# State-space phase: order and buffering of the gate units' store, powers of the scan in PSUM, large levels in two pieces

## The chip, the cores and the metric

One Trainium2 chip; the kernel runs on one core of it. The metric is the device time of one execution in microseconds (us). Five engines take part: PE (TensorE: matmuls, with its weight loads shown as PEld), DVE (VectorE), ACT (ScalarE), POOL (GpSimd) and SP (SyncE), which here does nothing but wait on semaphores and issue DMA transfers in a fixed order.

## What is computed

The reference is a model of two blocks on 256 tokens of width 1024. The change lies in one part of the first block, its second layer, an S5 state-space mixer over 256 context tokens and then 256 tokens, in both directions:

```python
def s5_scan(u, abar, bbar, cmat, h0):            # per chunk of the sequence
    def step(h, u_blk):
        bu = jnp.einsum('btgn,gpn->btgp', u_blk.astype(jnp.complex64), bbar)
        bu = bu.at[:, 0].add(abar[None] * h)
        a = jnp.broadcast_to(abar, bu.shape)
        _, hs = lax.associative_scan(_linrec_combine, (a, bu), axis=1)   # h[t] = abar * h[t-1] + bu[t]
        y = jnp.einsum('btgp,gnp->btgn', hs, cmat).real
        return hs[:, -1], y
```

`u` is one half of a projection of the modulated, normalised input (`s5_w_in`, 1024 x 4096); the other half, z, goes through SiLU and later multiplies the mixer's output (after GELU and a gated linear unit). There are 128 groups of 16 channels with 64 complex states each. All is fp32: a product is made from three matmuls, lead x lead, lead x rest and rest x lead, where `lead` is the operand rounded to the matmul's format (an ACT copy) and `rest` what remains (a DVE or POOL subtraction).

## The kernel before, in words

`s5_mixer` (from line 1538) runs the phase as five programs, one for each engine, tied together by semaphores. All five count the same steps n = 0 to 26 (`STEPS` = 27), and the order of work inside a step is written out by hand. The 16 channel tiles (k = 0 to 15, 128 channels each) run through a pipeline of stages that lie some steps apart:

- Step n below 16: TensorE projects unit n of u (`project`, L1767: 8 x 3 matmuls of 128x512) into `ps_u`; ACT copies it to `us`; SP stores it and loads it back turned as `ub`. Steps 16 to 23: the units are the gate's z, two units of 256 columns in a step (`gate_half`, 24 matmuls each), both into `ps_u`; ACT puts them through SiLU into `zb` (L1962), and SP stores `zb` (L1687). The unit's weights come from the ring: ACT makes `w_lead` (`lead`, L1885), DVE `w_rest` (`rest`, L1990), two buffers of each.
- Step n, tile n - 2 (`BACK`): TensorE makes the states' inputs (L1868) into `ps_s`, ACT spreads them into `S` (L1955 to L1957).
- Tile n - 9 (`LAG`): TensorE makes the lag kernels (L1790 to L1803) from V, which POOL builds (L1751 to L1753, twelve instructions for a tile) or, for five tiles, SP loads; ACT evicts them (L1921), SP turns them by four loads into T (L1668).
- Tile n - 10 (`OUT`): ACT copies the scanned states to `hs` (`states`, L1900, L1901), TensorE makes the outputs (L1819) from hs, V, T and `ul`; every second tile ACT applies GELU, every fourth step TensorE turns four tiles (`turn_outputs`) and ACT copies them on (`gate_inputs`).

The scan itself is DVE's. The tiles go in four quarters q = 0 to 3 of four tiles; `scan(q, part)` runs parts 0 to 3 in steps 6 + 4q to 9 + 4q. A scan goes up and down a tree of 5 levels over 64 chunk states; each move is one `advance` with four instructions: L2001 and L2002 multiply states by powers of abar (real part; imaginary part with crossed components), L2003 adds the two into `t1`, L2004 adds the sum to the states.

`apow` (powers), `S` (states) and `t2` lie in SBUF, `t1` in PSUM (two banks). A scan's advances have, in order, 1024, 960, 960, 448, 192, 64, 64, 128, 256, 512 and 1024 elements per partition, 5632 together. Between the two halves of parts 0 to 2, and behind both halves of part 3, stand the `w_rest` of the next step's units. `scanned` is raised at a scan's end, and ACT's `states` of the quarter wait for it.

SP's order in a step before: store of u, T loads (behind the lag eviction of this step), loads of W and ub, the units' weights, and only then the store of z of the step before; ACT's SiLU waits for that store, as `zb` is one buffer.

The phase begins with `ModulatedParts`: eight tiles of the input are turned by TensorE into a ring of PSUM banks (L628), ACT makes `h_lead` (L635), DVE the value (L645), POOL `h_rest` (L652). The ring has six banks, four borrowed from `ps_s` and `ps_y` and two from `t1`; the tiles that don't fit are turned between the matmuls of unit 0.

## Time and profile before

| | |
|---|---|
| time, median of 3 runs | 1713.45 us (1709.28, 1713.45, 1713.57) |
| the profiled execution | 1709.84 us, span 1707.8 us |
| busy: PE, PEld, DVE, ACT, POOL | 91%, 78%, 58%, 46%, 39% |
| granted TensorE clock, mean | 0.952 of full speed |
| the state-space phase | about 553 to 899 us of the span |
| moved by DMA | 328.8 MB, mean 193 GB/s |

The durations used below come from the profiled execution, whose times count from the start of its span. "Granted clock" is the share of full speed that TensorE was given in a stretch. "Idle before" is the time in which an engine did nothing before an instruction, with the instruction that ended the wait.

### The profile page before, as it was taken

The numbers are of one execution on the slowest core, as the hardware profiler recorded it, in microseconds if no ns is written. First come the engines' busy times: TensorE is split into PE (matmuls) and PEld (weight loads), VectorE is DVE, ScalarE is ACT, GpSimd is POOL, SyncE is SP. The second block draws the span as 40 slices with busy tenths as digits, with TensorE's granted clock in tenths as the row PEclk, the third lists the DMA queues.
The fourth block names the chain that finished last, engine by engine and source line by source line (L and its number), as shares of the span: only waits on it lengthen the run. The fifth ranks groups of instructions, "written<-read, shape, count | busy, mean of one in ns | idle before, by whom it ended". The sixth has DMA issues, their size and how long they took to land. (4 is left out here: it accounts for less than half of the span.)

```text
span 1707.8 us, 28308 instructions
## 1 busy us (share of the span) xinstructions
PE 1552.7 (91%) x11434; PEld 1327.3 (78%) x11434; DVE 995.4 (58%) x1271; ACT 791.2 (46%) x1064; POOL 664.3 (39%) x505
## 2 busy tenths in 40 slices
PE   4799999799699899998579998989999999899998
PEld 0478888588688788787569987778999967689997
DVE  6444532388735358669826645564766655557665
ACT  2422222365412577675354434554545464455452
POOL 0089994599698943478902015111000000110000
PEclk9889999999899999989779999889999999899999
DMA  9976775466534677877657455315535333245531
GB/s 386 427 273 230 247 251 192 143 194 194 202 125 169 179 251 195 226 209 224 154 152 273 173 187 185 148 50 198 222 149 220 123 114 148 99 162 209 220 149 50
DMA packets 119289, 328.80 MB, mean 193 GB/s; under 512 B 33396, under 2 KB 72692, under 8 KB 102920
## 3 DMA queue, kind: packets, MB, share of 16 engines
q1 hardware_dynamic: 116310, 301.71, 51.7%
q10 hardware_dynamic: 2868, 25.54, 4.2%
q8 instruction: 79, 1.29, 0.3%
q14 instruction: 32, 0.26, 0.1%
HBM read 282.17 MB, written 36.65 MB: 187 GB/s over the span
## 5 line engine op out<-in xcount | busy, mean ns | idle before, releaser
L3033 PE MATMUL ffn_ps<-ffn_x_lead,w_lead 128*128 128x256 f32 x672 | 188.4, 280 | 1.1 <-DVE w_rest L3112 1.1
L3033 PE MATMUL ffn_ps<-ffn_x_lead,w_rest 128*128 128x256 f32 x672 | 188.6, 281 | 0.0
L3033 PE MATMUL ffn_ps<-ffn_x_rest,w_lead 128*128 128x256 f32 x672 | 188.3, 280 | 0.0
L401 POOL TENSOR_TENSOR w_rest<-resident_ring,w_lead 128x2048 fp32r<-128x2048 f32 x7 | 32.1, 4590 | 394.9 <-ACT w_lead L397 206.3
L3112 DVE TENSOR_TENSOR w_rest<-resident_ring,w_lead 128x2048 fp32r<-128x2048 f32 x42 | 96.1, 2292 | 83.7 <-ACT w_lead L3077 83.7
L365 PE MATMUL qkvz_ps<-qkvz_w_lead,h_lead 128*128 128x512 f32 x320 | 125.8, 393 | 5.8 <-POOL h_rest L652 5.8
L3033 PEld LDWEIGHTS ffn_ps<-ffn_x_lead,w_lead 128*128 128x128 f32 x672 | 126.1, 188 | 2.2 <-issue 1.4
L3033 PEld LDWEIGHTS ffn_ps<-ffn_x_rest,w_lead 128*128 128x128 f32 x672 | 126.4, 188 | 0.7
L3033 PEld LDWEIGHTS ffn_ps<-ffn_x_lead,w_rest 128*128 128x128 f32 x672 | 126.3, 188 | 0.0
L365 PE MATMUL qkvz_ps<-qkvz_w_lead,h_rest 128*128 128x512 f32 x320 | 125.4, 392 | 0.0
L365 PE MATMUL qkvz_ps<-qkvz_w_rest,h_lead 128*128 128x512 f32 x320 | 125.4, 392 | 0.0
L1767 PE MATMUL ssm_ps_u<-h_lead,w_lead 128*128 128x512 f32 (+1 forms) x256 | 94.1, 368 | 33.8 <-DVE w_rest L1990 22.8
L282 DVE TENSOR_TENSOR qkvz_w_rest<-resident_ring,qkvz_w_lead 128x2048 fp32r<-128x2048 f32 x20 | 55.4, 2771 | 118.6 <-ACT qkvz_w_lead L276 118.6
L282 DVE TENSOR_TENSOR w_rest<-resident_ring,w_lead 128x2048 fp32r<-128x2048 f32 x33 | 77.3, 2344 | 71.0 <-ACT w_lead L276 70.6
L276 ACT ACTIVATE qkvz_w_lead<-resident_ring 128x2048 fp32r<-128x2048 f32 x20 | 38.5, 1923 | 149.1 <-PE qkvz_ps L365 146.9
L1428 POOL TENSOR_TENSOR resident_x<-xc,resident_x 128x512 f32<-128x512 f32 x64 | 104.9, 1640 | 5.0
L3077 ACT ACTIVATE w_lead<-resident_ring 128x2048 fp32r<-128x2048 f32 x42 | 80.1, 1912 | 50.6 <-PE ffn_ps L3033 50.5
L276 ACT ACTIVATE w_lead<-resident_ring 128x2048 fp32r<-128x2048 f32 x33 | 63.2, 1914 | 85.5 <-PE odd_ps L365 28.5
L1990 DVE TENSOR_TENSOR w_rest<-resident_ring,w_lead 128x1024 fp32r<-128x1024 f32 x32 | 48.3, 1515 | 82.7 <-ACT w_lead L1885 81.8
L1767 PE MATMUL ssm_ps_u<-h_rest,w_lead 128*128 128x512 f32 (+1 forms) x256 | 89.9, 351 | 0.0
L1767 PE MATMUL ssm_ps_u<-h_lead,w_rest 128*128 128x512 f32 (+1 forms) x256 | 89.8, 351 | 0.0
L1767 PEld LDWEIGHTS ssm_ps_u<-h_lead,w_lead 128*128 128x128 f32 x256 | 52.7, 206 | 45.8 <-issue 30.2
(534 smaller groups left out, 4506.7 us busy)
## 6 DMA issues: line engine op xcount, KB each, us to landing
resident_ring<-in_ffn_gu SPq DMA_DIRECT2D x22, 2048.0 KB, 9.0
ffn_wd<-in_ffn_down SPq DMA_DIRECT2D x22, 1024.0 KB, 4.9
resident_ring<-in_ada_w SPq DMA_DIRECT2D x8, 2048.0 KB, 13.3
xc<-s_q_scratch SPq DMA_DIRECT2D x128, 128.0 KB, 3.4
resident_x<-in_s_bT SPq DMA_DIRECT2D x64, 256.0 KB, 3.9
resident_ring<-in_attn_w_in ACTq DMA_DIRECT2D x8, 2048.0 KB, 10.4
s_W_scratch<-resident_x SPq DMA_DIRECT2D x64, 256.0 KB, 2.9
resident_ring<-in_s_w SPq DMA_DIRECT2D x32, 512.0 KB, 6.4
```

Of the source, the lines that this page charges most:

```text
L276: self.core.nc.scalar.activation(self.w[0][j], self.core.tile(r)[:, j * HK:(j + 1) * HK, :], ACT.Copy).then_inc(self.lead_made, 1)
L282: self.core.nc.vector.tensor_tensor(self.w[1][j], self.core.tile(r)[:, j * HK:(j + 1) * HK, :], self.w[0][j].bitcast(F32), ALU.subtract).t ...
L365: last = nc.tensor.matmul(bank(parity, t), self.lhs[x][:, half * HK + k, t * P:(t + 1) * P], self.w[w][j][:, k, :], start=(half, k, x, w) ...
L401: self.core.nc.gpsimd.tensor_tensor(self.slots[1][0], self._raw(r), self.slots[0][0].bitcast(F32), ALU.subtract).then_inc(self.rest_made, 1)
L1428: g.tensor_tensor(b, q(0), b, ALU.mult).then_inc(self.scaled, 1)
L1767: last = nc.tensor.matmul(out, w[:, s, k, :], hparts[x][:, k, cols], start=k == 0 and x == 0 and w is w_lead, stop=k == KT - 1 and w is w_ ...
L1990: v.tensor_tensor(w_rest[:, u % 2], raw, w_lead[:, u % 2].bitcast(F32), ALU.subtract).then_inc(rest_made, 1)
L3033: last = nc.tensor.matmul(ps[s][f][:, m, :], w_part[w][m][:, k, f * P:(f + 1) * P], x_part[x][:, k, :], start=(k, w, x) == (0, 0, 0), stop ...
L3077: nc.scalar.activation(w_part[0][m], raw(s, m), ACT.Copy).then_inc(w_lead_made, 1)
L3112: v.tensor_tensor(w_part[1][m], raw(s, m), w_part[0][m].bitcast(F32), ALU.subtract).then_inc(w_rest_made, 1)
```

## The change

It has three parts. The store of z moves to the head of SP's step, in front of the T loads, and gets a second buffer, which is `us[0]` in odd steps; SiLU then waits for the store of two steps before. The powers of a quarter are copied by ACT from SBUF to a PSUM tile (`powers`, one bank, single-buffered) before the quarter's scan, and DVE reads them there. And an advance with more than 8 positions (512 elements) runs as two pieces, so that `t1` has half its size and one bank; the ring of `ModulatedParts` has five banks with that.

```diff
--- before.py
+++ after.py
@@ -1551,8 +1551,8 @@
         S = nc.alloc_sbuf_tensor_at("ssm_S", [P, 2, 2, NCH, QG], F32, offset=low)
-        t2 = ph.sb("t2", [P, 2, LC // 2, QG])
-        apow = ph.sb("apow", [P, 2, LEVELS, 3, QG])
+        t2 = ph.sb("t2", [P, 2, LC // 4, QG])
+        apow_raw = ph.sb("apow", [P, 2, LEVELS, 3, QG])
         hs = ph.sb("hs", [P, 2, QG, LC])
@@ -1563,14 +1563,15 @@
         gb = ph.sb("gb", [P, 4, NL])
-        zb = ph.sb("zb", [P, 2, NL])
+        zb = [ph.sb("zb", [P, 2, NL])[:], us[0][:].rearrange("p t n -> p (t n)").rearrange("p (i n) -> p i n", i=2)]
         vt = ph.sb("vt", [P, 512])
...
         ps_u = ph.ps("ps_u", [P, NTOK])
-        t1 = ph.ps("t1", [P, 2, LC // 2, QG])
+        t1 = ph.ps("t1", [P, 2, LC // 4, QG])
+        apow = ph.ps("powers", [P, LEVELS, 3, QG])
         ps_s = [ph.ps(f"ps_s{h}", [P, 2, 4, NCH]) for h in range(2)]
@@ -1579,13 +1580,14 @@
         y_done, y_kept, turned, g_made, cleared, feed_made = [sem(n) for n in "y_done y_kept turned g_made cleared feed_made".split()]
-        g_stored, z_stored, feed_in = [sem(n) for n in "g_stored z_stored feed_in".split()]
+        g_stored, feed_in = [sem(n) for n in "g_stored feed_in".split()]
+        z_stored = [sem(f"z_stored{s}") for s in range(2)]
         T_landed = [sem(f"T_landed{s}") for s in range(2)]
...
         c_landed, V_landed = [[sem(f"{n}{s}") for s in range(4)] for n in ("c_landed", "V_landed")]
-        behind_done = sem("behind_done")
+        behind_done, powers_kept = sem("behind_done"), sem("powers_kept")
         LOADED = EarlyQuads.TILES
@@ -1598,7 +1600,7 @@
         mod = ModulatedParts(core, ph, 1, xc, hparts, [m[:].rearrange(o) for m, o in ((ps_s[0], "p c g n -> p (c g n)"), (ps_s[1], "p c g n -> p (c g n)"),
-                                                                                      (ps_y[0], "p g n -> p (g n)"), (ps_y[1], "p g n -> p (g n)"))] + [t1[:, i].rearrange("p s g -> p (s g)") for i in range(2)],
+                                                                                      (ps_y[0], "p g n -> p (g n)"), (ps_y[1], "p g n -> p (g n)"))] + [t1[:].rearrange("p i s g -> p (i s g)")],
                              [hs[:].rearrange("p c g s -> p (c g s)")[:, i * NTOK:(i + 1) * NTOK] for i in range(4)])
@@ -1624,7 +1626,7 @@
                 def apow_load(q):
-                    sp.dma_start(apow[:, q % 2], d["s5_a"][:, q]).then_inc(apow_in[q % 2], 16)
+                    sp.dma_start(apow_raw[:, q % 2], d["s5_a"][:, q]).then_inc(apow_in[q % 2], 16)
 
@@ -1654,6 +1656,10 @@
                     k, kl = n - OUT, n - LAG
+                    done = units(n - 1)
+                    if done and done[0] >= CT:
+                        sp.wait_ge(z_made, n - CT)
+                        sp.dma_start(d["z"][done[0] - CT:done[-1] - CT + 1].rearrange("u p n -> p u n"), zb[(n - 1) % 2]).then_inc(z_stored[(n - 1) % 2], 16)
                     if is_ct(n - 1):
@@ -1681,10 +1687,6 @@
                             s5_unit_load(core, sp, u + 4)
-                    done = units(n - 1)
-                    if done and done[0] >= CT:
-                        sp.wait_ge(z_made, n - CT)
-                        sp.dma_start(d["z"][done[0] - CT:done[-1] - CT + 1].rearrange("u p n -> p u n"), zb[:]).then_inc(z_stored, 16)
                     if k == 11:
@@ -1720,7 +1722,8 @@
                     gate_load(core, sp, u)
-                sp.wait_ge(z_stored, 16 * (CT // 2))
+                for s in range(2):
+                    sp.wait_ge(z_stored[s], 16 * (CT // 4))
 
@@ -1900,6 +1903,12 @@
 
+                def powers(q):
+                    act.wait_ge(apow_in[q % 2], 16 * (q // 2 + 1))
+                    if q:
+                        act.wait_ge(scanned, q)
+                    sc.activation(apow[:], apow_raw[:, q % 2], ACT.Copy).then_inc(powers_kept, 1)
+
                 def gate_inputs(k):
@@ -1921,6 +1930,8 @@
                         gate_inputs(k - 1)
+                    if (n - BACK - 4) % 4 == 0 and 0 <= (n - BACK - 4) // 4 < NQ:
+                        powers((n - BACK - 4) // 4)
                     if is_ct(k) and k % 4 == 0:
@@ -1957,9 +1968,11 @@
                         act.wait_ge(z_done, 2 * (n - CT) + 2)
-                        if n > CT:
-                            act.wait_ge(z_stored, 16 * (n - CT))
-                        sc.activation(zb[:].rearrange("p i n -> p (i n)"), ps_u[:], ACT.Silu).then_inc(z_made, 1)
+                        if n >= CT + 2:
+                            act.wait_ge(z_stored[n % 2], 16 * ((n - CT) // 2))
+                        if n == CT + 1:
+                            act.wait_ge(u_stored[0], 16 * (CT // 2))
+                        sc.activation(zb[n % 2].rearrange("p i n -> p (i n)"), ps_u[:], ACT.Silu).then_inc(z_made, 1)
                     if len(following) > 1:
@@ -1992,21 +2005,25 @@
                     at = S[:, q % 2]
+                    if count > LC // 4:
+                        advance(q, level, first, step, LC // 4)
+                        advance(q, level, first + step * (LC // 4), step, count - LC // 4)
+                        return
                     stop = first + step * (count - 1) + 1
...
                     a, b = t1[:, :, 0:count, :], t2[:, :, 0:count, :]
-                    v.tensor_tensor(a, apow[:, q % 2, level, 0, :].unsqueeze(1).unsqueeze(1).to_broadcast(shape), of, ALU.mult)
-                    chain.run(v.tensor_tensor(b, apow[:, q % 2, level, 1:3, :].unsqueeze(2).to_broadcast(shape), of[:, ::-1], ALU.mult))
+                    v.tensor_tensor(a, apow[:, level, 0, :].unsqueeze(1).unsqueeze(1).to_broadcast(shape), of, ALU.mult)
+                    chain.run(v.tensor_tensor(b, apow[:, level, 1:3, :].unsqueeze(2).to_broadcast(shape), of[:, ::-1], ALU.mult))
                     chain.run(v.tensor_tensor(a, a, b, ALU.add))
...
                         dve.wait_ge(s_kept, 8 * (q + 1))
-                        dve.wait_ge(apow_in[q % 2], 16 * (q // 2 + 1))
+                        dve.wait_ge(powers_kept, q + 1)
                         advance(q, 0, 1, 2, CC // 2)
```

SP, steps 17 and 18 of the phase, before (T loads alternate between `ssm_T_odd` and `resident_x`; `in_s_w` are the units' weights):

```order
L1668 DMA resident_x<-ssm_lags 128x1x256 x4
L1515 DMA resident_ring<-in_s_w 128x1024 x2
L1687 DMA z_scratch<-ssm_zb 128x2x256
L1618 DMA ssm_b_all<-s_bb_scratch 128x2x128
L1621 DMA ssm_cc<-in_s_cA 128x256
L1632 DMA ssm_V<-s_V_scratch 128x1024 x2
L1624 DMA ssm_ptab<-s_p_scratch 128x512
L1668 DMA ssm_T_odd<-ssm_lags 128x1x256 x4
L1515 DMA resident_ring<-in_s_w 128x1024 x2
L1687 DMA z_scratch<-ssm_zb 128x2x256
```

and with the change:

```order
L1662 DMA z_scratch<-ssm_zb 128x2x256
L1674 DMA resident_x<-ssm_lags 128x1x256 x4
L1515 DMA resident_ring<-in_s_w 128x1024 x2
L1620 DMA ssm_b_all<-s_bb_scratch 128x2x128
L1623 DMA ssm_cc<-in_s_cA 128x256
L1634 DMA ssm_V<-s_V_scratch 128x1024 x2
L1626 DMA ssm_ptab<-s_p_scratch 128x512
L1662 DMA z_scratch<-ssm_us 128x2x256
L1674 DMA ssm_T_odd<-ssm_lags 128x1x256 x4
L1515 DMA resident_ring<-in_s_w 128x1024 x2
```

The z store has moved past four T loads and two weight loads; every second one now reads `ssm_us`.

DVE, the start of a quarter's scan, before:

```order
L2001 TENSOR_TENSOR ssm_t<-ssm_apow,ssm_S 128x1024
L2002 TENSOR_TENSOR ssm_t<-ssm_apow,ssm_S 128x1024
L2003 TENSOR_TENSOR ssm_t<-ssm_t 128x1024
L2004 TENSOR_TENSOR ssm_S<-ssm_S,ssm_t 128x2x16x32
L1990 TENSOR_TENSOR w_rest<-resident_ring,w_lead 128x1024
```

and with the change:

```order
L2018 TENSOR_TENSOR ssm_t<-ssm_powers,ssm_S 128x512
L2019 TENSOR_TENSOR ssm_t<-ssm_powers,ssm_S 128x512
L2020 TENSOR_TENSOR ssm_t<-ssm_t 128x512
L2021 TENSOR_TENSOR ssm_S<-ssm_S,ssm_t 128x2x8x32
L2018 TENSOR_TENSOR ssm_t<-ssm_powers,ssm_S 128x512
L2019 TENSOR_TENSOR ssm_t<-ssm_powers,ssm_S 128x512
L2020 TENSOR_TENSOR ssm_t<-ssm_t 128x512
L2021 TENSOR_TENSOR ssm_S<-ssm_S,ssm_t 128x2x8x32
L2003 TENSOR_TENSOR w_rest<-resident_ring,w_lead 128x1024
```

Eight instructions of 512 elements stand in front of the subtraction instead of four of 1024, and the powers come from the tile that ACT fills.

ACT, with the change, from the SiLU of step 17 (its output is now `ssm_us`) to the first `states` of step 18:

```order
L1975 ACTIVATE ssm_us<-ssm_ps_u 128x512
L1888 ACTIVATE w_lead<-resident_ring 128x1024
L1983 ACT_TABLE_LOAD
L1983 ACTIVATE resident_x<-ssm_ps_y 128x4x8x16
L1930 ACTIVATE ssm_lags<-ssm_ps_l 128x2x240
L1910 ACTIVATE ssm_powers<-ssm_apow 128x480
L1903 ACTIVATE ssm_hs<-ssm_S 64x2x256
L1904 ACTIVATE ssm_hs<-ssm_S 64x2x256
```

The row L1910 is new; the rest of the order is as before.

## Rows read from the trace of the kernel before

**Rows 1.** Busy time by stretch: us, then each engine's busy us, clock, DMA share, GB/s.
```profile
584.00:617.00 33.00, 33.00 (x212) 29.61 (x211) 5.36 (x3) 25.28 (x39) 31.75 (x26) 1.00 0.82 241
617.70:652.50 34.80, 32.99 (x297) 28.93 (x295) 33.57 (x47) 22.23 (x36) 0.84 (x1) 1.00 0.60 182
...
766.00:888.00 122.00, 86.31 (x1669) 80.08 (x1656) 84.25 (x81) 65.30 (x77) 80.67 (x53) 0.84 0.66 166
789.70:852.90 63.20, 44.74 (x857) 41.30 (x856) 53.94 (x51) 26.41 (x33) 58.59 (x39) 0.82 0.66 169
854.40:879.50 25.10, 25.09 (x496) 23.22 (x496) 3.45 (x3) 13.80 (x16) 0.00 (x0) 0.90 0.44 96
```
**Rows 2.** PE's waits, 553 to 900 us: waiting <- awaited: us in total, times, longest.
```profile
PE ssm_ps_u L1767 <- DVE w_rest L1990: 22.8, 5, 10.6
...
PE ssm_ps_u L1767 <- ACT ssm_zb L1962: 6.2, 1, 6.2
...
PE ssm_ps_u L1767 <- POOL h_rest L652: 2.5, 6, 1.2
```
**Rows 3.** PE in order of time: start, us, instruction, [idle before <- releaser].
```profile
635.11 0.47 PE L1767 MATMUL ssm_ps_u<-h_lead,w_lead 128*128 128x512 f32 x1 [1.20 <-DVE w_rest L1990]
...
685.17 1.65 PE L1790 MATMUL ssm_ps_l<-ssm_V,ssm_b_all 64*32 64x112 f32 x32 [3.07 <-issue]
...
787.75 0.55 PE L1767 MATMUL ssm_ps_u<-h_lead,w_lead 128*128 128x256 f32 x1 [7.22 <-DVE w_rest L1990]
...
854.41 0.55 PE L1767 MATMUL ssm_ps_u<-h_lead,w_lead 128*128 128x256 f32 x1 [10.61 <-DVE w_rest L1990]
...
888.16 1.08 PE L1819 MATMUL ssm_ps_y<-ssm_V,ssm_hs 128*32 128x128 f32 x16 [8.66 <-issue]
```
**Rows 4.** ACT's waits, 766 to 899 us.
```profile
ACT ssm_zb L1962 <- DMA z_scratch<-ssm_zb: 20.1, 4, 6.6
```
**Rows 5.** ACT in order of time.
```profile
816.87 0.61 ACT L1921 ACTIVATE ssm_lags<-ssm_ps_l 128x480 f32<-128x480 f32 x1
...
830.83 1.28 ACT L1962 ACT_TABLE_LOAD   x1 [9.66 <-DMA z_scratch<-ssm_zb]
...
877.40 0.60 ACT L1962 ACTIVATE ssm_zb<-ssm_ps_u 128x512 f32<-128x512 f32 x1 [4.44 <-DMA z_scratch<-ssm_zb]
```
**Rows 6.** SP's queue in order of time: start, us to issue, transfer.
```profile
817.51 4.12 SPq L1668 DMA_DIRECT2D ssm_T_odd<-ssm_lags  x4
...
823.85 0.45 SPq L1687 DMA_DIRECT2D z_scratch<-ssm_zb  x1
```
**Rows 7.** DVE by line and shape, 617 to 657 us (POOL silent): busy us, mean ns.
```profile
L1990 DVE TENSOR_TENSOR w_rest<-resident_ring,w_lead 128x1024 fp32r<-128x1024 f32 x4 | 4.9, 1225 | 0.2
L2001 DVE TENSOR_TENSOR ssm_t<-ssm_apow,ssm_S 128x1024 f32<-128x1024 f32 x2 | 3.1, 1574 | 6.2 <-ACT ssm_S L1957 6.2
L2003 DVE TENSOR_TENSOR ssm_t<-ssm_t 128x1024 f32<-128x1024 f32 x2 | 2.5, 1232 | 0.1
...
L2002 DVE TENSOR_TENSOR ssm_t<-ssm_apow,ssm_S 128x1024 f32<-128x1024 f32 x2 | 2.4, 1214 | 0.0
...
L2003 DVE TENSOR_TENSOR ssm_t<-ssm_t 128x512 f32<-128x512 f32 x1 | 0.7, 700 | 0.0
```
**Rows 8.** DVE by line and shape, 766 to 853 us (POOL beside it).
```profile
L1990 DVE TENSOR_TENSOR w_rest<-resident_ring,w_lead 128x1024 fp32r<-128x1024 f32 x10 | 16.9, 1699 | 9.5 <-ACT w_lead L1885 9.2
L2002 DVE TENSOR_TENSOR ssm_t<-ssm_apow,ssm_S 128x1024 f32<-128x1024 f32 x3 | 6.4, 2127 | 0.0
...
L2003 DVE TENSOR_TENSOR ssm_t<-ssm_t 128x1024 f32<-128x1024 f32 x3 | 3.7, 1232 | 0.1
```
**Rows 9.** POOL's subtraction for V: 665 to 686 us, then 584 to 592 us.
```profile
L1753 POOL TENSOR_TENSOR ssm_V<-ssm_V,ssm_vt 128x512 f32<-128x512 f32 x4 | 7.0, 1746 | 0.3
...
L1753 POOL TENSOR_TENSOR ssm_V<-ssm_V,ssm_vt 128x512 f32<-128x512 f32 x3 | 3.8, 1282 | 0.2
```
**Rows 10.** DVE in order of time, the subtractions for step 18.
```profile
785.81 4.01 DVE L1990 TENSOR_TENSOR w_rest<-resident_ring,w_lead 128x1024 fp32r<-128x1024 f32 x2
```

## The prediction

> **What bounds the kernel now.** I read the page first, then the busy time by stretch, then who waited for whom, then the instructions in order of time around each wait. The whole program is TensorE's: it is busy 91% of the 1707.8 us. The state-space phase (553 to 899 us) is not quite that. In its first steps TensorE has no gap at all (33.00 us of 33), but from 766 to 888 us, where the gate units run, it is busy for 86.3 of 122 us at a granted clock of 0.84 [rows 1]. So there are some 35 us to be had in that stretch, and what ends each wait says how. TensorE waits 22.8 us for DVE's `w_rest` and 6.2 us, once, in step 21, for ACT's `zb` [rows 2]. In order of time the large waits for `w_rest` are 7.22 us in step 18 and 10.61 in step 22, and 8.66 us pass before the last outputs [rows 3].
>
> Two chains lie behind them. The first is the store of z. ACT's SiLU of a step waits until the store of the step before has landed: 20.1 us in four waits directly in front of it [rows 4], and more in front of its table load. Step 20 to 21 shows it: ACT evicts the lag kernels at 816.87, SP issues the four loads of T from 817.51, then two unit loads, and only at 823.85 the z store of a buffer that was filled before all this; ACT goes on at 830.83, after 9.66 us idle, with the table load [rows 5, 6]. That is 30 us of idle time on ACT. The second is DVE's scan. Where POOL is silent its multiplication with the powers takes 1214 ns for 1024 elements, the same as the addition from PSUM at 1232 [rows 7]; where POOL builds V beside it, it takes 2127, while the additions stay what they were [rows 8]. What differs is the operands: L2001 and L2002 read powers and states both from SBUF, L2003 and L2004 read one from SBUF and one from PSUM. The subtractions L1990, two SBUF inputs too, average 1699. The scan of quarter 0 fills DVE from 617.7 to 652.5 without idle time; less three subtractions of 1.23 us and 0.7 us for contention in its first instruction (two L2001 of mean 1574 instead of 1232 [rows 7]) that is 30.4 us. Quarter 3 takes 63.2 us, less 8.2 us idle and six subtractions of 1.70: 44.8 us [rows 1, 8]. Its subtractions stand between the scan's pieces, and TensorE waits for them.
>
> **The change, part by part** (against the profiled execution's own 1709.84 us).
>
> *Five banks for the modulated input instead of six.* Tile 5 is turned later, behind the matmuls of tile 2, which wait for POOL's h_rest. TensorE waits 2.5 us for h_rest now, 1.2 us at the longest [rows 2]. POOL's eight h_rest follow each other in one chain, so tile 5 costs only what it comes too late for its turn in it. No row shows that: I take +0.5 us, between 0 (hidden by POOL's chain) and +1.2 (one more of the longest waits).
>
> *Powers to PSUM.* Four ACT copies of 128x480, each like the eviction of the lags, 0.61 us [rows 5]. They stand on ACT in steps 6, 10, 14 and 18 in front of `states`, and DVE's scan now waits for them: 0.6 us later at its start in step 6, up to 1.2 in steps 10 and 14, where a lag eviction stands in front too. Behind the copy on ACT stand `states` and the next w_lead, 0.6 us later; TensorE does not wait for either in steps 6, 10 and 14 now. The copy also waits for the scan before to end; ACT gets there after it in steps 10 and 14, and in step 18 `states` waits for the same.
>
> *Two pieces.* A piece of 512 takes 0.70 per instruction against 1.23 for 1024 [rows 7], so a divided advance takes 8 x 0.70 = 5.6 instead of 4 x 1.23 = 4.9: +0.7 us, four times a quarter, +2.8. A scan without contention is then 33.2 us.
>
> *Quarter 0, no POOL beside.* Nothing is won, and TensorE already waits 1.20 us for a subtraction in step 8 [rows 3]. In front of it lie one copy (+0.6), three divided advances (+2.0), and the contended 0.7 us of the first instruction that goes: +1.9 us. Bounds 1.0 (the copy hidden, a little less per piece) and 2.8 (the 0.7 us stay).
>
> *Quarter 1, POOL beside.* TensorE waits 3.07 us at 685.17 for V of tile 3 [rows 3], twelve POOL instructions between 665 and 686 us. POOL suffers as DVE does: L1753 takes 1746 ns there, 1282 where DVE is quiet [rows 9]. Some 19.5 us x (1 - 1282/1746) = 5.2 us are contention; even if two contended subtractions keep their part, more than 3.07 us go. Late next is TensorE itself (the states of step 11). Behind a wait the clock is low for a while: a 128x256 matmul behind the wait of step 18 shows 0.55 us [rows 3]. I take -5 us; between -3 (the wait alone) and -6 (all the slow matmuls behind it too).
>
> *Gate units.* The z store now goes out at the head of SP's next step, in front of the T loads, 0.45 us of queue for them; it waits for the SiLU, which ACT does before the lags the T loads wait for, so it holds nothing up. With two buffers the SiLU waits for a store two steps old, and ACT's 30 us of waits go. Late next is DVE. Its two subtractions for step 18 begin at 785.8 [rows 10], behind the last 1984 of scan 2's 5632 elements. These take 35% of a scan: 0.35 x 44.8 = 15.8 us now, 0.35 x 30.4 + 0.7 = 11.4 then, so they begin at 781.4. DVE's queue from there: two subtractions (2.5 instead of 4.0), scan 3 (33.2), six subtractions (between 1.23 and 1.70 each [rows 7, 8], I take 8.8 us together), and waits for w_lead, 8.2 us now, of which the z waits in steps 18 and 20 made most. The second unit's w_lead still has to wait for TensorE's second half and the SiLU, so I leave 4.5 us. 781.4 + 2.5 + 33.2 + 8.8 + 4.5 + 1.2 = 831.6 is when the first subtraction for step 22 is done, where TensorE now goes on at 854.41 [rows 3]: -22.8 us. TensorE alone would be there earlier: it runs from 854.4 to 879.5 without a gap, two steps and a half in 25.1 us [rows 1], so four steps from 783 end near 823. It still waits 6 to 9 us for DVE in step 22. Behind it, up to 879.5, nothing changes; the last SiLU loses its 4.44 us wait [rows 5], which brings the last lags, and by them the last T loads and outputs, forward by some 1.6 us (TensorE's own last lags, done near 878, bound it then). Together -24.4. Bounds: -28 (subtractions uncontended, TensorE at the full clock) and -17 (all subtractions at 1.70, all 8.2 us of waits stay).
>
> On the price of a PSUM operand rule and row differ. The row: +0.02 us per instruction, 1232 with one operand from PSUM against 1214 with none [rows 7]. The Trainium skill ("VectorE: DVE Perf Modes", the section on the TRN2 errata) gives a fixed part of 120 cycles from PSUM against 58 from SBUF; at its 0.96 GHz that is an estimate of 0.065 us for each of the 42 multiplications between step 17 and step 22, 2.7 us, and the forecast would be that much later. I go by the row.
>
> Sum: 0.5 + 1.9 - 5 - 24.4 = -27.0 us. From the profiled execution's time that gives 1682.8, from the median of the three runs (1713.45; the profiled one lies at their low end, 1709.28) 1686.5. I take **1685**. All else follows in one piece: the GLU phase starts at a barrier and its loads are issued before that, earlier by the same.
>
> **The rivals.**
>
> *B, contention stays.* If what slows DVE is not the second SBUF operand but, say, POOL's use of the states' memory, z alone is won: DVE's idle 8.2 us shrink to 2, -6.2; the tail -1.6; against that the five divided advances from step 17 on, +3.5, quarter 0 +2.6, the start +0.5. Together -1.2: 1712. For it: no row shows a multiplication with a PSUM operand broadcast. Against it: L2003 and L2004 do not slow down. 12%.
>
> *C, a transfer takes the place.* The stretch 766 to 888 has a DMA share of 0.66 [rows 1]; in 98 us it would be 0.82. The four T loads of a step take 4.1 us to issue [rows 6] and land after that; with steps of 10 us there is little time left before the outputs that read them. If landing takes 4 us more, four steps and the last outputs pay 3 each, +14: 1699. Against it: at a share of 0.82 (584 to 617 us) TensorE had no gap [rows 1]. 11%.
>
> *D, slower.* The multiplications have never read their powers, repeated along two axes, out of PSUM. They are half of the scan, 16.6 of 33.2 us. If each takes f times as long, the chain to step 22 gets 23 x (f - 1) longer and quarter 0, where three pieces stand before a subtraction that TensorE waits for, some 8 x (f - 1). 27 / 31 = 0.9: the gain is gone at f = 1.9, 2.3 us for 1024 elements. At f = 2.5: +34 + 12 - 27 = +19, and ACT stands at the next quarter's copy until the scan is over, some 5 us more: 1737. The gain needs f below that, and the rows show 1.0 for a PSUM operand that is read straight through. 5%.
>
> *A, my forecast*: 72%, between 1677 (best bounds, from the lowest run) and 1697 (worst bounds, from the highest).
>
> **How the numbers follow.** 1685 is case A's. The range 1676 to 1705 takes in A and C and leaves out B, D and a few per cent of A. About 0.3% (5 us) is what a measurement can tell from no change here: A and C are faster, B mostly the same, D slower. Faster 0.85, same 0.10, slower 0.05.
>
> **What would show it.** Right: multiplications of 512 elements near 0.70 us in the stretch with POOL beside, no ACT wait on the z store, no TensorE wait before L1790 near 685 us, step 8's wait for w_rest near 3 us, one TensorE wait of 6 to 9 us in step 22, the phase's last outputs near 860 us. Wrong: multiplications over 0.9 us beside POOL (B), waits in front of the outputs in steps 19 to 23 (C), or 512-element multiplications over 1 us already in quarter 0 (D).

## The result, and the profile after

The changed kernel takes 1686.06 us, the median of four runs (1685.76 to 1691.57), beside 1713.51 us, the median of four of the kernel before (1709.28 to 1720.78). The ratio is 0.985, with a 95% interval from 0.9827 to 0.9872: 27.4 us less, where the forecast was 1685 against 1713.45. A second comparison, of six executions with eleven, gave 1689.94 us (1686.41 to 1693.2) against 1711.4, a ratio of 0.9873 (0.9843 to 0.9902): 21.5 us less. The profiled execution took 1686.28 us, with a span of 1684.5 and a mean granted clock of 0.96.

First the stretches that answer to [rows 1], the busy time of each engine by window in the changed kernel:

```profile
core 0: us, PE busy (x) PEld busy (x) DVE busy (x) ACT busy (x) POOL busy (x), PEclk, DMA share, GB/s
584.00:617.00 33.00, 33.00 (x211) 29.63 (x210) 5.25 (x3) 24.18 (x37) 31.75 (x26) 1.00 0.79 245
617.00:652.50 35.50, 33.52 (x291) 29.17 (x289) 31.83 (x59) 24.11 (x39) 1.04 (x1) 0.95 0.56 181
766.00:860.00 94.00, 79.77 (x1550) 73.99 (x1549) 63.25 (x97) 62.20 (x74) 67.41 (x51) 0.92 0.75 204
```

The stretch with the gate units, up to the last outputs, is some 94 us long instead of 122. TensorE's share of it and its clock are both higher: the granted clock is 0.92 instead of 0.84, the busy share 85% instead of 71%. The DMA share is 0.75 instead of 0.66.

Who waits for whom between 553 and 900 us, as in [rows 2]:

```profile
PE ssm_ps_y L1822 <- issue: 10.1, 3, 6.1
PE ssm_ps_u L1770 <- DVE w_rest L2003: 9.8, 4, 5.6
PE ssm_ps_u L1770 <- POOL h_rest L652: 5.5, 6, 2.3
PE ssm_ps_s L1841 <- ACT ssm_S L1968: 2.7, 1, 2.7
```

The waits for w_rest have gone from 22.8 us to 9.8 and the one for zb is no longer there; those for h_rest have grown from 2.5 to 5.5. In order of time, TensorE's instructions behind a wait (start, length, and in brackets the wait), the first at the phase's start, the others as in [rows 3]:

```profile
558.23 0.47 PE L1770 MATMUL ssm_ps_u<-h_lead,w_lead 128*128 128x512 f32 x1 [2.32 <-POOL h_rest L652]
...
637.90 0.47 PE L1770 MATMUL ssm_ps_u<-h_lead,w_lead 128*128 128x512 f32 x1 [0.91 <-DVE w_rest L2003]
...
684.78 0.40 PE L1793 MATMUL ssm_ps_l<-ssm_V,ssm_b_all 64*32 64x112 f32 x8
...
779.59 0.45 PE L1770 MATMUL ssm_ps_u<-h_lead,w_lead 128*128 128x256 f32 x1 [2.21 <-DVE w_rest L2003]
...
831.20 0.56 PE L1770 MATMUL ssm_ps_u<-h_lead,w_lead 128*128 128x256 f32 x1 [5.58 <-DVE w_rest L2003]
...
861.68 0.64 PE L1822 MATMUL ssm_ps_y<-ssm_V,ssm_hs 128*32 128x128 f32 x6 [6.12 <-issue]
```

The wait in front of step 18 is 2.21 us instead of 7.22, in front of step 22 5.58 instead of 10.61, in front of the last outputs 6.12 instead of 8.66. The wait of 3.07 us in front of the lag kernels of tile 3 is gone. POOL, which builds V for them, became faster too, 664 to 687 us; in [rows 9] its subtraction took 1746 ns, and its product into `vt` took 1433 in the same stretch:

```profile
L1756 POOL TENSOR_TENSOR ssm_V<-ssm_V,ssm_vt 128x512 f32<-128x512 f32 x4 | 5.1, 1286 | 0.3
L1755 POOL TENSOR_TENSOR ssm_vt<-ssm_ptab,ssm_cc 128x512 f32<-128x512 f32 x4 | 4.4, 1111 | 0.0
```

DVE's instructions by line and form, 764 to 832 us, where POOL builds V beside them (as in [rows 8]):

```profile
L2003 DVE TENSOR_TENSOR w_rest<-resident_ring,w_lead 128x1024 fp32r<-128x1024 f32 x11 | 17.9, 1642 | 10.6 <-ACT w_lead L1888 10.3
L2020 DVE TENSOR_TENSOR ssm_t<-ssm_t 128x512 f32<-128x512 f32 x10 | 7.0, 700 | 0.3
L2018 DVE TENSOR_TENSOR ssm_t<-ssm_powers,ssm_S 128x512 f32<-128x512 f32 x10 | 7.0, 697 | 0.3
L2021 DVE TENSOR_TENSOR ssm_S<-ssm_S,ssm_t 128x512 f32<-128x512 f32 x10 | 6.9, 687 | 0.3
L2019 DVE TENSOR_TENSOR ssm_t<-ssm_powers,ssm_S 128x512 f32<-128x512 f32 x10 | 6.8, 680 | 0.0
```

The multiplications (L2018, L2019) now take no longer than the additions (L2020, L2021). The subtractions still take 1642 ns: both their inputs are still in SBUF. ACT's waits between 764 and 885 us hold no line with z_scratch any more (20.1 us in [rows 4]). What remains in front of the SiLU (L1975, into `ssm_zb` or `ssm_us`) is its own input:

```profile
ACT w_lead L1888 <- PE ssm_ps_u L1770: 14.5, 6, 3.9
ACT ssm_us L1975 <- PE ssm_ps_u L1770: 5.9, 3, 2.9
...
ACT ssm_zb L1975 <- PE ssm_ps_u L1770: 4.0, 3, 1.9
```

**The phase by itself.** The rest of the program varies from execution to execution by more than most effects below: the phase's first transposition started between 553.5 and 558.9 us in the 14 profiles of this study. So every profile is also read from that transposition (L628) on. In microseconds from there; "step 18" and "step 22" are the first matmul of these steps' gate units, "S" is the turn of outputs that waits for the states near 732 us in the kernel before, and "GLU" the first matmul of the next phase (step 22 is blank where the order around it was changed):

| kernel | unit 2 | step 8 | S | step 18 | step 22 | last outputs | GLU |
|---|---|---|---|---|---|---|---|
| before | 23.3 | 79.8 | 177.2 | 232.5 | 299.1 | 332.9 | 341.4 |
| changed | 26.1 | 84.4 | 177.3 | 226.1 | 277.7 | 308.1 | 316.7 |
| changed_again | 26.6 | 84.9 | 178.1 | 229.2 | 277.8 | 308.5 | 317.0 |
| z_only | 23.3 | 79.8 | 176.3 | 231.3 | 293.0 | 323.5 | 332.1 |
| powers_only | 26.1 | 84.4 | 180.2 | 229.7 | 292.6 | 326.5 | 336.0 |
| pieces_only | 23.3 | 81.8 | 177.0 | 235.0 | 301.9 | 336.0 | 344.6 |
| quiet_pool | 24.0 | 80.0 | 176.7 | 226.0 | 289.3 | 322.9 | 331.4 |
| powers_in_sbuf | 26.0 | 83.9 | 180.4 | 237.5 | 303.3 | 334.2 | 343.7 |
| z_and_quiet_pool | 23.3 | 79.8 | 177.0 | 226.4 | 276.3 | 307.1 | 316.5 |
| z_one_buffer | 26.1 | 84.4 | 175.4 | 225.1 | 275.4 | 306.8 | 316.3 |
| z_store_late | 26.6 | 84.9 | 175.9 | 225.7 | 275.8 | 308.0 | 317.5 |
| six_banks | 23.3 | 81.6 | 174.9 | 225.6 | 274.9 | 306.3 | 315.8 |
| rests_early | 23.3 | 81.7 | 173.9 | 224.5 | | 305.6 | 315.0 |
| rests_early_alone | 25.9 | 84.2 | 175.3 | 225.3 | | 307.6 | 317.0 |

The change takes 24.7 us out of the phase in the one profile and 24.4 in the other. These are single profiles. The two of the changed kernel agree within 0.9 us everywhere but at step 18, where they are 3.1 apart, so a difference of 3 us at one point of this table shows nothing by itself. The same holds from step 8 to S: the eight kernels with the powers in PSUM have the same code there and took 91.0 to 95.8 us.

### The profile page after: what moved, and what is told of

It reads as the page before. It is cut to its first block and busy times, and to the rows that moved or that the text cites. A ratio compares the mean times of both kernels' runs of the same rounds, so it can differ in the third digit from the quotient of the medians.

```text
span 1684.5 us, 28380 instructions
## 1 busy us (share of the span) xinstructions
PE 1549.4 (92%) x11434; PEld 1323.6 (79%) x11434; DVE 961.2 (57%) x1335; ACT 792.9 (47%) x1068; POOL 645.4 (38%) x505
## 5 line engine op out<-in xcount | busy, mean ns | idle before, releaser
L282 DVE TENSOR_TENSOR qkvz_w_rest<-resident_ring,qkvz_w_lead 128x2048 fp32r<-128x2048 f32 x20 | 51.3, 2563 | 123.0 <-ACT qkvz_w_lead L276 123.0
L1754 POOL TENSOR_TENSOR ssm_V<-ssm_ptab,ssm_cc 128x512 f32<-128x512 f32 x36 | 46.7, 1298 | 90.0 <-PE ssm_ps_y L1822 87.6
```

What stands on the lines that cost most here:

```text
L282: self.core.nc.vector.tensor_tensor(self.w[1][j], self.core.tile(r)[:, j * HK:(j + 1) * HK, :], self.w[0][j].bitcast(F32), ALU.subtract).t ...
L1754: g.tensor_tensor(v, power(c), coef(0), ALU.mult)
```

## The experiments

The theory on trial: two things held the gate units up, DVE's scan slowed by POOL and ACT's wait for the store of z, the scan being the larger; the powers' place in PSUM takes POOL's part away, the pieces only cost. The rivals: one of the two was the real bound; it was the shorter instructions that helped; or DMA traffic rather than POOL slows DVE.

### The halves of the change

**z_only**: the kernel before with the z edits alone.

```
+ sp.dma_start(d["z"][...], zb[(n - 1) % 2])      (first in SP's step, two buffers)
  apow in SBUF, advances undivided, six banks      (as before)
```

> The kernel before with the z edits alone: the store of z at the head of SP's step and two buffers; powers in SBUF, undivided advances, six banks. Theory (two separate causes, DVE's contended scan the larger): the scan keeps its 44.8 us in quarter 3, DVE loses 4 to 6 of its 8.2 us of waits for w_lead, the last outputs come some 1.6 us earlier by themselves; -6 to -9 us against the kernel before, some 1706. ACT shows no wait on z_scratch, TensorE still waits 8 to 12 us for w_rest in step 22. Rival (the store's wait was TensorE's real bound and the scan only looked like it): -15 to -20 us, 1695, and the wait in step 22 shrinks below 6 us.

Measured: 1707.16 us against 1712.17, ratio 0.9969 (0.9941 to 0.9997), 5.0 us less; the phase is 9.3 us shorter, where 6 to 9 had been expected. ACT waits for no store. TensorE's waits for w_rest are as they were, 10.65 us in step 22:

```profile
PE ssm_ps_u L1769 <- DVE w_rest L1994: 24.6, 6, 10.7
```

DVE's own idle time is what went. Its wait for w_lead between 785 and 850 us is 0.2 us, 8.2 in the kernel before. But with the steps closer together more of its work meets POOL: a subtraction takes 1906 ns on average instead of 1699. The stretch from step 18 to step 22 is 61.8 us instead of 66.7. The theory holds; its rival, 15 us or more from the store alone, falls.

**powers_only**: the changed kernel with the z edits undone.

```
- sp.dma_start(d["z"][...], zb[(n - 1) % 2])      (first in SP's step, two buffers)
+ sp.dma_start(d["z"][...], zb[:])                 (behind the unit loads, one buffer)
```

> The changed kernel with the z edits undone: powers in PSUM, divided advances and five banks stay; z has one buffer again and its store stands behind the T loads and unit loads. Theory: -27 without the tail's 1.6 and the 3.7 us of waits for w_lead, so near -20 against before, some 1693; if the two parts overlap, because a faster DVE runs into ACT's waits for the store, only -12 to -18 (1695 to 1701), and ACT's waits in front of zb stay at 15 us or more. Rival (the store was the real bound): -7 or less, 1706 or above. Multiplications of 512 beside POOL 0.70 us by either.

Measured: 1706.74 us, ratio 0.9976 (0.9954 to 0.9998), 5.4 us less, and 5.4 us less in the phase. The multiplications of 512 beside POOL take 696 and 679 ns, so DVE's work is as short as in the changed kernel. It gains little of it, since it now stands and waits. ACT's and DVE's waits between 764 and 885 us:

```profile
ACT ssm_zb L1971 <- DMA z_scratch<-ssm_zb: 17.8, 4, 6.8
ACT L1971 <- DMA z_scratch<-ssm_zb: 16.6, 3, 9.1
```

```profile
DVE w_rest L1999 <- ACT w_lead L1886: 30.9, 6, 9.9
```

ACT waits 34.4 us for the store of z (32.8 in the kernel before), w_lead comes behind that, and DVE's subtractions wait for w_lead: 16.9 us of it between 785 and 850 us, twice the 8.2 of the kernel before. The expectation of 1695 to 1701 "if the two parts overlap" was still too low. The time is the one that the rival had named, 1706 or above, but its claim that the store alone was the bound falls with z_only. Neither fault by itself was the bound.

**quiet_pool**: the kernel before with POOL's V instructions cut to an eighth of their elements from tile 4 on, z as it was. It leaves out seven eighths of V for these tiles.

```
+ few = (lambda m: m[:, :, 0:1]) if k >= 4 else (lambda m: m)
+ g.tensor_tensor(few(v), few(power(c)), few(coef(0)), ALU.mult)      (and the two behind it)
```

> The kernel before with POOL's instructions for V cut to one eighth of their elements from tile 4 on (seven eighths of these tiles' V are not computed; nothing else is left out). Theory (DVE is slow because POOL's V instructions run beside it): multiplications of 1024 elements take 1.21 us everywhere, subtractions for w_rest 1.23, the wait of 3.07 us for V goes; the time falls by 20 us or more (1693 or below), though ACT's waits for the z store stay at 15 to 20 us. Rival (DMA traffic of these stretches slows DVE): multiplications stay above 1.8 us between 766 and 853 us, and only the 3 to 5 us of the wait for V go.

Measured: 1706.83 us, ratio 0.9976 (0.9959 to 0.9994). DVE by line and form, 764 to 853 us:

```profile
L1991 DVE TENSOR_TENSOR w_rest<-resident_ring,w_lead 128x1024 fp32r<-128x1024 f32 x12 | 14.7, 1232 | 27.2 <-ACT w_lead L1886 26.8
L2003 DVE TENSOR_TENSOR ssm_t<-ssm_apow,ssm_S 128x1024 f32<-128x1024 f32 x3 | 3.8, 1261 | 0.0
...
L2002 DVE TENSOR_TENSOR ssm_t<-ssm_apow,ssm_S 128x1024 f32<-128x1024 f32 x3 | 3.7, 1231 | 0.1
```

What the theory says of the cause is right: with POOL nearly silent the same instructions, with the same operands in SBUF and a DMA share of 0.75 in the stretch, take 1231 and 1261 ns instead of 1987 and 2127 (L2001 and L2002 of the kernel before), and the subtractions 1232 instead of 1699. The DMA rival falls: the share was 0.66 in the kernel before. What it says of the time is wrong: 5.3 us less instead of 20 or more. DVE idles 26.8 us for w_lead, and behind it stands the store of z. Taking POOL's work away gives what moving the powers gives, some 5 us. The wait of 3.06 us in front of the lag kernels of tile 3 stays, as it must: tile 3's V is built in full here, and DVE and POOL contend there as before.

**z_and_quiet_pool**: the same with the z edits.

> The kernel before with the z edits, and POOL's instructions for V cut to one eighth of their elements from tile 4 on (seven eighths of these tiles' V are not computed). Powers in SBUF, undivided advances, six banks. Each of the two alone gave some 5 us (1707.2 and 1706.8 against 1712.2). Theory (two chains of nearly the same length stood behind TensorE, each hid what the other gave; and PSUM for the powers does nothing but take away POOL's interference): 1677 to 1685, at or below the changed kernel, with no TensorE wait over 4 us in step 22. Rival (the gains add, and the large gain comes from something else in the change): 1700 to 1703.

Measured: 1690.68 us (1681.11 to 1694.26), ratio 0.9858 (0.9817 to 0.99). The phase takes 316.5 us, 24.9 less than before and as long as the changed kernel's; the longest wait for w_rest is 3.80 us. The median is above the 1677 to 1685 that were expected, and far from the 1700 to 1703 of the rival. (That the phase is just as long as the changed kernel's is in part chance: this kernel has six banks and undivided advances, and the wait of 3.06 us for V is still there.) So the table of two by two, in phase lengths: 341.4 with neither, 332.1 with the z edits, 336.0 with the powers' half, 316.7 with both. The two gains alone sum to 14.7 us; together they are 24.7. In the times the gains alone are 5.0 and 5.4 us, together 21.5 or 27.4. With the quiet POOL in place of PSUM: 341.4, 332.1, 331.4, 316.5.

Where the extra 10 us come from is seen between steps 18 and 22. The kernel before takes 66.7 us there. The faster scan alone saves 44.8 - 32.8 = 12.0 us of DVE's work (the changed kernel's scan 3 goes from 781.42 to 829.1 us, 47.7 us, less six subtractions of 9.0 and 5.9 of waits), but its waits for w_lead grow from 8.2 to 16.9: 66.7 - 12.0 + 8.7 = 63.4, and 62.8 were measured. The z edits alone take 8.0 us of waits away: 58.7, and 61.8 were measured; six slower subtractions (11.9 us instead of 10.1) are 1.8 of the 3.1 us between. Both: 66.7 - 12.0 - 2.3 = 52.4, and 51.6 were measured (48.6 in changed_again, whose step 18 came later).

### What the second half hangs on

**pieces_only**: the kernel before with the divided advances alone.

```
+ if count > LC // 4:
+     advance(q, level, first, step, LC // 4)
+     advance(q, level, first + step * (LC // 4), step, count - LC // 4)
+     return
```

> The kernel before with the divided advances alone (powers in SBUF, six banks, z as it was). Theory (the pieces only cost; what helps is the operand's place): +2.0 us in quarter 0, +3.5 to +5 from step 17 on, together +4 to +7 against before, 1718 to 1720; multiplications of 512 beside POOL take 1.1 to 1.2 us. Rival (shorter instructions suffer less from POOL): multiplications of 512 near 0.75 us beside POOL too and a time below the kernel before, -10 or more.

Measured: 1718.64 us, ratio 1.0044 (1.0026 to 1.0062), 6.5 us more; step 8 comes 1.9 us later, for which 2.0 had been worked out. Multiplications of 512 beside POOL, 764 to 853 us, take twice the 700 and 684 ns that they take in quiet_pool:

```profile
L2006 DVE TENSOR_TENSOR ssm_t<-ssm_apow,ssm_S 128x512 f32<-128x512 f32 x9 | 12.5, 1389 | 0.0
L2005 DVE TENSOR_TENSOR ssm_t<-ssm_apow,ssm_S 128x512 f32<-128x512 f32 x9 | 12.2, 1353 | 0.2
```

Shorter ones suffer no less than long ones, and more than the 1.1 to 1.2 us expected. In time the pieces are a price and nothing else.

**powers_in_sbuf**: the changed kernel with the powers read from SBUF.

```
- powers((n - BACK - 4) // 4)                      (ACT's copy)
...
- v.tensor_tensor(a, apow[:, level, 0, :]...
+ v.tensor_tensor(a, apow_raw[:, q % 2, level, 0, :]...        (and the line behind it)
```

> The changed kernel with DVE reading the powers from SBUF again and no copies on ACT; divided advances, five banks and the z edits stay. Theory (the operand's place is what the second half of the gain hangs on): multiplications of 512 take 1.3 to 1.4 us beside POOL, as in the kernel with the pieces alone (1353 and 1389 ns), TensorE waits 10 us or more for w_rest in step 22; time z_only's 1707 plus the pieces' 6, some 1710 to 1714. Rival (the z edits and the pieces carry it): below 1695.

Measured: 1716.8 us, ratio 1.0026 (1.0007 to 1.0044), above the 1710 to 1714 expected. DVE between 764 and 862 us:

```profile
L2001 DVE TENSOR_TENSOR w_rest<-resident_ring,w_lead 128x1024 fp32r<-128x1024 f32 x12 | 21.0, 1772 | 2.5 <-ACT w_lead L1888 2.1
L2017 DVE TENSOR_TENSOR ssm_t<-ssm_apow,ssm_S 128x512 f32<-128x512 f32 x10 | 14.6, 1457 | 0.0
L2016 DVE TENSOR_TENSOR ssm_t<-ssm_apow,ssm_S 128x512 f32<-128x512 f32 x10 | 12.4, 1237 | 0.3
L2018 DVE TENSOR_TENSOR ssm_t<-ssm_t 128x512 f32<-128x512 f32 x10 | 7.0, 700 | 0.3
L2019 DVE TENSOR_TENSOR ssm_S<-ssm_S,ssm_t 128x512 f32<-128x512 f32 x10 | 6.9, 687 | 0.3
```

L2016 and L2017 have one operand elsewhere than L2018 and L2019 of the changed kernel, and take 1237 and 1457 ns where those take 697 and 680. One step of TensorE waits 14.7 us for w_rest. The operand's place is worth some 27 us once the z edits are in, and without it the whole change is a loss.

### Which half of the z edit

**z_one_buffer**: the changed kernel with a single buffer, the store first.

```
- zb = [ph.sb("zb", [P, 2, NL])[:], us[0][:].rearrange(...)]
+ zb = [ph.sb("zb", [P, 2, NL])[:]] * 2
...
+ act.wait_ge(z_stored[(n - 1) % 2], 16 * ((n - 1 - CT) // 2 + 1))
```

> The changed kernel with one buffer for z instead of two; the store stays at the head of SP's step. Theory (the late issue of the store was the fault, not the single buffer): the store of a step is issued 1 us behind its SiLU and lands 5 to 8 us later, the next SiLU comes 10 us later, so ACT waits 0 to 2 us in all and the time is that of the changed kernel, 1685 to 1689. Rival (the second buffer is needed): ACT waits 8 us or more for the store in all, and the time is 1692 or more.

**z_store_late**: the changed kernel with two buffers, the store back behind the T and unit loads.

> The changed kernel with two buffers for z, but the store back behind the T and unit loads. Theory: the store of a step is issued some 7 us late and has a further 10 us until its buffer is wanted, so ACT waits for it 3 us or less in all; the T loads start half a us earlier; time 1685 to 1690. Rival (the place in SP's queue decides, a late store is late for two steps too, or holds up loads behind it): 1695 or more.

Measured: z_one_buffer 1689.25 us, ratio 0.9873 (0.9842 to 0.9904), phase 316.3; z_store_late 1685.61 us, ratio 0.9846 (0.9822 to 0.9871), phase 317.5. In neither does ACT wait for a store. In z_one_buffer the store is issued 0.6 to 3.4 us behind its SiLU's start and the next SiLU waits for TensorE alone:

```profile
805.54 0.60 ACT L1973 ACTIVATE ssm_zb<-ssm_ps_u 128x512 f32<-128x512 f32 x1 [1.53 <-PE ssm_ps_u L1770]
815.29 0.60 ACT L1973 ACTIVATE ssm_zb<-ssm_ps_u 128x512 f32<-128x512 f32 x1 [0.24 <-PE ssm_ps_u L1770]
```

```profile
806.17 0.38 SPq L1662 DMA_DIRECT2D z_scratch<-ssm_zb  x1
```

Either half does the whole: an early store or a second buffer. The faults were needed together, a late store and one buffer.

### The start, and a try for more

**changed_again**: the changed kernel beside the next three. Its 1689.94 us, given above, are 1 us over the range expected here.

> The changed kernel as it is, beside the next three, for a comparison on one chip: 1684 to 1689.

**six_banks**: the bank of the powers is lent to the modulated input before step 6.

```
- apow = ph.ps("powers", [P, LEVELS, 3, QG])
+ powers_bank = ph.ps("powers", [P, NTOK])
+ apow = powers_bank[:, 0:LEVELS * 3 * QG].rearrange("p (l c g) -> p l c g", l=LEVELS, c=3)
...
- ... + [t1[:].rearrange("p i s g -> p (i s g)")],
+ ... + [t1[:].rearrange("p i s g -> p (i s g)"), powers_bank[:]],
```

> The changed kernel with the bank that holds the powers from step 6 on lent to the modulated input before that, so six banks instead of five. Theory (the sixth bank's loss costs more than the 0.5 us that I gave it): from the phase's first transposition to the start of unit 2 TensorE takes 23.3 us instead of 26.1, and the time is 2 to 3 us below the changed kernel. Rival (that difference is chance, or POOL's chain hides it later): within 0.5 us of the changed kernel, and 26 us to the start of unit 2.

Measured: 1689.76 us, ratio 0.9864 (0.9834 to 0.9893), beside 1689.94 of the changed kernel on the same chip. Unit 2 starts at 23.3 us from the phase's start, as in the kernel before. So the 2.8 us go with the fifth bank, though not with it alone: rests_early_alone has six banks and starts unit 2 at 25.9. At the GLU phase 0.9 to 1.3 us of them are left, and the time shows none of the 2 to 3 us expected. How the 2.8 us are made up stands in the busy time by window, unit 1 in the changed kernel and in this one:

```profile
571.12:579.64 8.52, 7.32 (x24) 5.58 (x25) 1.57 (x1) 1.92 (x4) 8.21 (x7) 0.80 0.57 185
```

```profile
573.63:580.50 6.87, 5.70 (x24) 4.42 (x25) 1.59 (x1) 1.89 (x4) 6.62 (x5) 1.00 0.64 198
```

The wait for h_rest in front of unit 0 is 2.32 us in the changed kernel, 0.22 here; unit 1 starts 1.2 us later, and its granted clock is 0.80 instead of 1.00, which is another 1.65 us.

**rests_early**: six banks, and in step 21 DVE makes both w_rest in front of the scan's last advance; TensorE does both halves of step 22 in front of the outputs.

```
+ elif q == NQ - 1:
+     advance(q, 1, 33, 4, 8)
+     between()
+     advance(q, 0, 32, 2, 16)
+     dve.sem_inc(scanned, 1)
...
+ if n == CT + 6:
+     gate_half(units(n)[1], 1)            (in front of outputs(k))
```

> Six banks as above; besides, DVE makes the two w_rest for step 22 in front of the last advance of the scan of quarter 3 (two pieces of 2.8 us), and TensorE does both gate halves of step 22 in front of the outputs of tile 12. In the changed kernel DVE reaches that point at 823.6 us, w_lead for the second unit is done at 824.9, the scan ends at 829.2 and TensorE goes on at 831.2. Then: both w_rest by 827.2, scan by 832.8, states of tile 12 by 835.1, outputs of tile 12 at 835.1 instead of behind both at 840.2 less 1.5: the turn 3.6 us earlier. Theory: 2 to 4 us below six_banks, and the wait of 5.6 us for w_rest becomes one of 1 us or less with one of 1 to 3 us for hs behind it. Rival (the T loads of tile 15 and what they wait for set the phase's end): within 1 us of six_banks, the last wait in front of L1822 longer by what is won.

**rests_early_alone**: the same without the change of TensorE's order.

> rests_early without the change of TensorE's order: outputs of tile 12 stand between the halves again. Theory: TensorE then waits 4 to 5 us for the states of tile 12 instead of 5.6 us for w_rest, and the time is within 1 us of six_banks. Rival: what is won by the earlier w_rest stays, 2 us or more below six_banks.

Measured: 1689.13 us (ratio 0.9869, 0.9839 to 0.99) and 1689.37 (0.9872, 0.9841 to 0.9903). Neither can be told from six_banks; 2 to 4 us had been expected of the first. Its wait for w_rest is gone and this one stands there, among TensorE's waits from 553 to 900 us:

```profile
PE ssm_ps_y L1823 <- ACT ssm_hs L1907: 3.8, 1, 3.8
```

The outputs of tile 12 begin 278.4 us from the phase's start, where six_banks has 280.3. Behind the wait the two halves of the lag kernels take 1.72 us each where they take 0.97 in six_banks, and at the GLU phase 0.7 us are left. Alone it turns a wait of 6.0 us for w_rest into one of 6.2 us for the states (4 to 5 had been expected):

```profile
PE ssm_ps_y L1823 <- ACT ssm_hs L1905: 6.2, 1, 6.2
```

Step 22 needs both the subtractions and the end of the scan from DVE, so their order hardly matters. No version tried here is measurably faster than the changed kernel.

## Why the prediction was right

**The sum**, term by term, from the table of the phase (the changed kernel less the kernel before):

| term | forecast | measured | from |
|---|---|---|---|
| five banks | +0.5 (0 to 1.2) | +2.8 | unit 2: 26.1 - 23.3 |
| quarter 0 | +1.9 (1.0 to 2.8) | +1.7 | step 8: +4.6, less 2.8 |
| quarter 1 | -5 (-3 to -6) | -4.5 | S: +0.1, less 4.6 |
| gate units | -24.4 | -24.8 | GLU: -24.7, less 0.1 |
| sum | -27.0 | -24.7 | |

The mechanism was right in the terms that carry the gain, the quarters and the gate units. That the time came within 1.1 us of 1685 was in part luck. The phase became 24.7 us shorter (24.4 in the other profile), not 27.0, and the second comparison gave 21.5 us. The 27.4 of the first lie above the phase's gain, and the prediction placed 1685 some 1.5 us below its own sum (1686.5). Worked from the profiled execution, the sum said 1682.8, and the profiled one took 1686.28. The -4.5 of quarter 1 is one draw from a stretch that took 91.0 to 95.8 us with the same code, 97.4 before.

**The mis-sized term** is the start. The prediction took the fifth bank's price from how long a wait for h_rest was, up to 1.2 us, and 1.2 us is by how much unit 1 did start later. It gave nothing for slower matmuls, though it had done so in quarter 1: 1.65 us in unit 1. The range of that term didn't hold the 2.8. Why the clock falls there is open. In four of the six profiles with five banks unit 0, right behind the wait of 2.3 us, ran at full clock, and the clock was low in unit 1, some 13 us later; between the two TensorE waited twice more for h_rest (1.23 and 1.24 us, against one such wait with six banks). The six profiles with five banks all have the first wait at 2.3 us and unit 1 at 7.3 us; of the eight with six banks, five have it at 0.2 to 0.5 us and unit 1 at 5.7 (the other three are told of at the end).

**Quarter 0 and quarter 1.** Step 8's wait for w_rest was to be near 3 us and was 0.91. Step 8 came 1.7 us later all the same, as forecast: TensorE had another 1.07 us of waits for w_rest at 626.19 and then a clock of 0.79 (626.2 to 634 us; 1.00 in the kernel before), so it arrived late by itself. In powers_only, where the clock was 1.00 there, it waited 2.50 us and step 8 began at the same 84.4. DVE sets that point, not TensorE. In quarter 1 POOL's part of the forecast is borne out: its subtraction for V went from 1746 to 1286 ns, with 1282 worked with in the prediction.

**The gate units.** DVE's first subtraction for step 18 was to begin 4.4 us earlier and began 6.0 us earlier, counted from the phase's start (3.7 in changed_again). The two took 3.43 us (2.5 forecast), the scan 32.8 without waits (33.2), six subtractions 9.0 (8.8), the waits for w_lead 5.9 (4.5; 2.5 in changed_again). TensorE went on at 831.20, and 831.6 had been worked out, but the two clocks don't match: the 831.6 leaves out the terms in front of it, and this profile's phase started 1.8 us earlier. What can be compared is the shift that the gate units made, -21.5 us up to step 22 where -22.8 was forecast. TensorE waited 5.58 us there; 6 to 9 had been said. The tail then lost more than the 1.6 us given to it, and the two errors cancel: from step 22 to the GLU phase 42.3 us before, 39.0 now, and 39.05 with the z edits alone, 43.5 with the powers' half alone. So it is z's, and it is 3.3 us: the wait in front of the last outputs fell from 8.66 to 6.12, and it is 8.7 to 9.0 us in all kernels without the z edits, 6.0 to 7.1 in all with them.

**How the 24.4 was shared out** was the weak point, though the sum needed no share. The working gave DVE's faster scan most of it and z the smaller part; rival B's sum has z alone at -7.8 us, and the phase showed -9.3. The powers' half alone I had put at 12 us or more before its run; it gave 5.4, with -2.7 at step 18 and -6.6 at step 22. What failed there was to take DVE's waits as given when DVE becomes faster: behind ACT's wait for the store they grew, from 8.2 us to 16.9 in powers_only, by most of the 12.0 that DVE saved.

**PSUM's price**: the row was right and the sentence from the Trainium skill ("VectorE: DVE Perf Modes", the section on the TRN2 errata, 120 cycles from PSUM against 58 from SBUF) is not borne out here. A multiplication of 512 elements with its powers in SBUF and no POOL beside it takes 700 and 684 ns in quiet_pool; with its powers in PSUM, repeated along two axes, 698 and 680 in the changed kernel between 617 and 652.5 us. There is no 0.065 us per instruction.

**The rivals.** B (contention stays) did not come; its price is shown by powers_in_sbuf, 1716.8 us where 1712 had been worked out. Its remark that POOL's use of the states' memory might be the cause is out: the states are still read and written in SBUF. C (transfers take the place): TensorE waits 1.99 us in front of outputs in step 19, for something that the profile doesn't name, not at all in front of those of steps 20 to 23, and 6.12 us in front of the last, less than before. So at a DMA share of 0.75 at most 2 of the 14 us came. D (PSUM broadcast slower): the factor f is 1.0.

## What to carry to other kernels

When two engines wait on each other in turn, as DVE and ACT do here, the gain of repairing one is not its busy time, and the gains don't add: here 9.3 and 5.4 us alone, 24.7 together. Before an edit is called worthless, ask what the engine it speeds up waits for next, and try it together with that. The vector operations with both inputs in SBUF paid for what GpSimd did beside them; moving one input to PSUM took them out of that, and here it was worth a copy and shorter instructions. When TensorE gets a new wait, look at the clock of the stretch behind it too, and not at the wait's length alone. And when a forecast hits, compare it term by term: here the start was off by 2.3 us and two errors inside the gate units cancelled, behind a time that was off by 1.1.

## What the runs showed of the hardware that was not expected

- GpSimd's interference was nearly all or nothing in these runs, by operand. Beside POOL a multiplication of 512 elements took 1237 to 1457 ns with two SBUF inputs and 680 to 697 with one of them in PSUM. With POOL's elements cut to an eighth (busy 21.5 of the 87 us from 766 to 853), though it still issued as many instructions, two SBUF inputs cost 1231 to 1261 ns for 1024 elements, near the 1214 with POOL silent. The Trainium skill ("SBUF — State Buffer", the section "Who interferes with whom") says that a DVE instruction with at most one SBUF input does not contend with GpSimd, and one with two contends with a GpSimd instruction that reads SBUF; the traces before and after agree. It gives no size for such a pair of instructions: here 75% on 1214 ns (2127, [rows 7, 8]), and on POOL's side 36% on 1282 ns (1746, [rows 9]).
- Unit 1 ran at a granted clock of 0.80 in all six profiles with a wait of 2.3 us in front of unit 0 (its matmuls from first to last took 7.3 us), and at full clock in the five with a wait of 0.2 to 0.5 us. With 1.9 us both were seen: unit 1 took 7.93 us in rests_early_alone, 5.70 in pieces_only and z_and_quiet_pool, which like it have six banks. All six are the kernels with five banks, so the first wait and the later ones can't be told apart, and no run shows which of them brings the low clock.
